# Both feed-forward products of a decoder layer by Strassen's scheme of seven block products

## What is computed

```python
hf = rmsnorm(x, norm_ffn_g[l])
gu = hf @ w_ffn_in[l]              # (1024 x 1024) @ (1024 x 5632)
gt, up = gu[..., :D_FF], gu[..., D_FF:]
x = x + (jax.nn.silu(gt) * up) @ w_ffn_out[l]   # (1024 x 2816) @ (2816 x 1024)
return rmsnorm(x, norm_final_g)
```

## Time and profile before

| | |
|---|---|
| median of 3 runs | 1623.27 us (1623.26 to 1623.52) |
| the profiled execution | 1621.26 us, of which 1619.4 us are the span from first to last instruction |
| TensorE busy | 1585.3 us, 98% of the span |
| VectorE, ScalarE, GpSimd busy | 651.1 us (40%), 450.5 us (28%), 128.9 us (8%) |
| feed-forward part | 867.0 us to the last matmul at about 1612.2 us |
| mean granted TensorE clock | 0.997 of full speed |

### The profile page before, as it was taken

The page is one execution under the profiler, slowest core; times in us unless marked ns, Lnnn a source line. Parts: engine busy times, 40 slices in busy tenths (PEclk is TensorE's granted clock), DMA queues, the critical chain, the costliest instruction groups (busy, mean ns, idle before and its releaser), DMA issues.

```text
span 1619.4 us, 18734 instructions
## 1 busy us (share of the span) xinstructions
PE 1585.3 (98%) x7640; PEld 1282.6 (79%) x7640; DVE 651.1 (40%) x916; ACT 450.5 (28%) x699; POOL 128.9 (8%) x141
## 2 busy tenths in 40 slices
PE   6999999999999999999999999999999999999998
PEld 5788888778787888887778888888888888888886
DVE  4162612666754323265636222414224142241426
ACT  5224112655643222154414211111111111111112
POOL 4000000000000002040002101010010100101002
PEclk9999999999999999999999999999999999999999
DMA  7223555323013525132011111111111111111102
GB/s 182 52 47 52 64 106 82 62 40 53 27 27 48 96 78 208 53 91 79 14 39 40 55 50 52 39 52 43 48 52 39 52 43 47 52 39 52 47 31 104
DMA packets 108538, 98.65 MB, mean 61 GB/s; under 512 B 3128, under 2 KB 90680, under 8 KB 108480
## 3 DMA queue, kind: packets, MB, share of 16 engines
q1 hardware_dynamic: 102720, 77.34, 21.2%
q0 software_dynamic: 4464, 15.77, 2.8%
q10 hardware_dynamic: 1296, 4.72, 0.7%
HBM read 89.40 MB, written 8.42 MB: 60 GB/s over the span
## 4 chain that ended last, share of the span: by engine, by line
PE 91%; DMA 2%; DVE 2%; ACT 2%; POOL 1%; issue 1%; SPq 0%; ACTq 0%; DVEq 0%; POOLq 0%
PE ps L1225 28%; PE ps L1226 28%; PE ps L1227 28%; PE ps L1475 2%; PE ps L1424 2%; PE ps L1455 1%; DMA za_dram<-za 1%; PE ps L1456 1%; DMA w_raw<-in_w_in 1%; PE ps L1232 1%; POOL w_lo L390 1%; ACT w_hi L474 0%; POOL rstd L382 0%; POOL ms L379 0%; DVE k L827 0%
## 5 line engine op out<-in xcount | busy, mean ns | idle before, releaser
L816 DVE TENSOR_TENSOR w_lo<-w_raw,w_hi 128x1024 fp32r<-128x1024 f32 (+1 forms) x124 | 151.5, 1222 | 674.2 <-ACT w_hi L474 673.0
L474 ACT ACTIVATE w_hi<-w_raw 128x1024 fp32r<-128x1024 f32 x132 | 139.4, 1056 | 882.8 <-PE ps L1227 868.8
L1225 PE MATMUL ps<-hf_lo,w_hi 128*128 128x512 f32 (+1 forms) x712 | 280.8, 394 | 0.1
L1227 PE MATMUL ps<-hf_hi,w_lo 128*128 128x512 f32 (+1 forms) x712 | 280.4, 394 | 0.0
L1226 PE MATMUL ps<-hf_hi,w_hi 128*128 128x512 f32 (+1 forms) x712 | 280.4, 394 | 0.0
L1225 PE MATMUL ps<-h_lo,w_hi 128*128 128x512 f32 (+1 forms) x456 | 183.7, 403 | 4.7 <-POOL w_lo L390 2.7
L1227 PE MATMUL ps<-h_hi,w_lo 128*128 128x512 f32 (+1 forms) x456 | 179.7, 394 | 0.0
L1226 PE MATMUL ps<-h_hi,w_hi 128*128 128x512 f32 (+1 forms) x456 | 179.4, 393 | 0.0
L1059 DVE TENSOR_TENSOR xr<-ps,xr 128x512 f32<-128x512 f32 x192 | 130.0, 689 | 88.4 <-PE ps L1227 88.4
L1225 PEld LDWEIGHTS ps<-hf_lo,w_hi 128*128 128x128 f32 x712 | 134.1, 188 | 32.1 <-issue 0.3
L1227 PEld LDWEIGHTS ps<-hf_hi,w_lo 128*128 128x128 f32 x712 | 134.1, 188 | 32.0
(11 more groups left out here) (218 smaller groups left out, 2120.7 us busy)
## 6 DMA issues: line engine op xcount, KB each, us to landing
w_raw<-in_w_ffn_in SPq DMA_DIRECT2D x44, 512.0 KB, 3.8
w_raw<-in_w_in SPq DMA_DIRECT2D x33, 512.0 KB, 7.8
w_raw<-in_w_ffn_out SPq DMA_DIRECT2D x22, 512.0 KB, 3.6
x_in<-in_x SPq DMA_DIRECT2D x8, 512.0 KB, 9.8
za_dram<-za ACTq DMA_DIRECT2D x8, 512.0 KB, 10.8
negc<-negc_dram POOLq DMA_DIRECT2D x8, 512.0 KB, 4.9
za_e<-za_dram POOLq DMA_DIRECT2D x8, 512.0 KB, 3.9
w_raw<-in_w_out SPq DMA_DIRECT2D x8, 512.0 KB, 3.6
```

Source lines behind the costliest of these rows:

```text
L474: nc.scalar.activation(w_hi[n % SLOTS][:, 0:w], w_raw[n % RAWS][:, 0:w], ACT.Copy).then_inc(hi_ready, 1)
L816: nc.vector.tensor_tensor(w_lo[n % SLOTS][:, 0:w], w_raw[n % RAWS][:, 0:w], w_hi[n % SLOTS][:, 0:w].bitcast(FP32), ALU.subtract).then_inc( ...
L1225: nc.tensor.matmul(dst, w_h, x_l, start=start, stop=False)
L1227: return nc.tensor.matmul(dst, w_l, x_h, start=False, stop=stop)
```

## The change

Both feed-forward products are cut into 2 x 2 blocks and made of seven block products for eight (Strassen's scheme, in the form with few additions). The contraction and the tokens are halved for the first product; for each of 22 column groups g of 256 (gate and up in turn) there are seven products P1, P2, P3, P7, P5, P6, P4 of 4 x 3 matmuls of 512 columns: 154 products, 1848 matmuls. For the second product there are seven sums over 11 steps, each step of 12 matmuls: 77 steps, 924 matmuls. 2772 matmuls in all.

- The token operands (B11, B21, B22 and the sums T3, T1, T2, T4) are formed once. GpSimd makes four sums for each of four pairs of token tiles, and TensorE transposes 28 units of four 128 x 128 tiles, 112 transposes, with GpSimd's `tok_t` and four PSUM banks in rotation.
- The weight operands: of seven for each g, three are quarters of the loaded pair and four are sums that GpSimd makes (`w_sums`), in one buffer `w_sum`. Each is split on ScalarE (`operand_hi`) and VectorE (`operand_lo`) seven products ahead, in a ring of ten slots.
- VectorE combines the seven results of each g (`evict`: seven operations that read PSUM), ScalarE copies P1 out. Silu and the product of gate and up work on SBUF (`silu_of`, `multiplied`). GpSimd makes four sums of the hidden quarters (`hidden_sums`), and SyncE stores seven quarters of 256 KB for each of 11 hidden blocks to DRAM (`store_hidden`, `hs_dram`). Before VectorE may overwrite `hq` for the next block, it waits for that store (`hs_stored`).
- The second product loads a hidden quarter (256 KB) for each of 77 steps (`load_hidden`, four buffers) and holds all of `w_ffn_out` in SBUF (`load_quad`); GpSimd makes 44 weight sums in place. Both operands of a step are split on ScalarE and VectorE (`split2_hi`, `split2_lo`); VectorE combines the seven sums (`evict2`, 48 operations of 128 x 512).
- The residual leaves SBUF: ScalarE issues eight stores of 512 KB while it squares (`xr_dram`) and four loads of 1 MB in the second product (`xf`).
- The hardware loops are gone; all steps are written out.

```diff
...
+OPS = ("B11", "B21", "B22", "T3", "T1", "T2", "T4")
+P1, P2, P3, P7, P5, P6, P4 = range(7)
+PAIRS_F = 2 * NJ
+ORDER = ([(0, P1), (0, P2), (1, P1), (1, P2)] + [(0, q) for q in range(2, 7)] + [(1, q) for q in range(2, 7)]
+         + [(g, q) for g in range(2, PAIRS_F) for q in range(7)])
+NTH = {gq: n for n, gq in enumerate(ORDER)}
...
+RING = 10
+LEAD = 7
...
+STEPS = PROD2 * NJ
+GROUPS = ((0, 4), (4, 8), (8, 11))
+SLOTS2 = 4
+BANKS2 = ((2, 3, 4, 6), (0, 1, 5, 7))
+T_AT = ("B11", "B22", "B12", "B12", "B11", "B12", "B21")
...
-            with sp.Fori(0, (NB - 1) // 2) as i:
-                for o in range(2):
-                    for r in range(6):
-                        n = base_of(1 + o) + r
...
+            def load_pair(g):
+                if g >= 2:
+                    sp.wait_ge(op_lo, NTH[g - 2, P4] + 1)
+                    sp.wait_ge(s_sum, 4 * (g - 2) + 4)
+                elif g == 1:
+                    sp.wait_ge(lo_ready, C_FF)
+                else:
+                    sp.wait_ge(xn_ready, N_FFN)
+                c0 = (g // 2) * 2 * P + (g % 2) * DFF
+                for half in range(2):
+                    view = w_ffn_in[half * HALF:(half + 1) * HALF, c0:c0 + 2 * P].rearrange("(k p) n -> p k n", p=P)
+                    sp.dma_start(raw_of(g, half)[:, :, :], view).then_inc(pair_in[g % 2][half], 16)
+            def store_hidden(j):
+                sp.wait_ge(hid_ready, 4 * (j + 1))
+                sp.dma_start(hs_dram[j, :, 0:3, :], hq[:, 0:3, :]).then_inc(hs_stored, 16)
+                sp.wait_ge(h_summed, 4 * (j + 1))
+                sp.dma_start(hs_dram[j, :, 3:7, :], h_sum[:]).then_inc(hs_stored, 16)
+            for g in range(PAIRS_F):
+                load_pair(g)
+                if g >= 5 and g % 2:
+                    store_hidden((g - 5) // 2)
+            store_hidden(NJ - 2)
+            def load_quad(q, i):
+                two_, col = {"B11": (0, 0), "B12": (0, 1), "B21": (1, 0), "B22": (1, 1)}[q]
+                sp.wait_ge(prod_done, N_PROD - {"B11": 5, "B22": 4, "B12": 1, "B21": 0}[q])
+                a, b = GROUPS[i]
...
+            def load_hidden(n):
+                i, k = divmod(n, NJ)
+                if n >= SLOTS2:
+                    sp.wait_ge(s_split, n - SLOTS2 + 1)
+                else:
+                    sp.wait_ge(op_lo, N_PROD)
+                    sp.wait_ge(s_sum, 4 * PAIRS_F)
+                sp.wait_ge(hs_stored, 32 * (k + 1))
+                sp.dma_start(s_raw(n % SLOTS2), hs_dram[k, :, S_AT[i], :]).then_inc(s_in[n % SLOTS2], 16)
+            ahead = {0: ("B11", 0), 2: ("B11", 1), 3: ("B11", 2), 4: ("B22", 0), 7: ("B22", 1), 9: ("B22", 2),
+                     12: ("B12", 0), 15: ("B12", 1), 18: ("B12", 2), 24: ("B21", 0), 28: ("B21", 1), 32: ("B21", 2)}
+            for n in range(STEPS):
+                if n == NJ - 1:
...
+            def w_sums(g):
+                for half in range(2):
+                    pool.wait_ge(pair_in[g % 2][half], 16 * (g // 2 + 1))
+                if g:
+                    pool.wait_ge(op_lo, NTH[g - 1, P6] + 1)
+                a11, a21 = raw_of(g, 0)[:, :, 0:P], raw_of(g, 0)[:, :, P:]
+                a12, a22 = raw_of(g, 1)[:, :, 0:P], raw_of(g, 1)[:, :, P:]
+                s3, s2, s4, s1 = (by_k(w_sum[:, i, :]) for i in range(4))
+                nc.gpsimd.tensor_tensor(s3, a11, a21, ALU.subtract).then_inc(s_sum, 1)
+                pool.wait_ge(s_sum, 4 * g + 1)
+                nc.gpsimd.tensor_tensor(s2, a22, s3, ALU.subtract).then_inc(s_sum, 1)
+                pool.wait_ge(s_sum, 4 * g + 2)
+                nc.gpsimd.tensor_tensor(s4, a12, s2, ALU.subtract).then_inc(s_sum, 1)
+                nc.gpsimd.tensor_tensor(s1, s2, a11, ALU.add).then_inc(s_sum, 1)
+            def hidden_sums(j):
+                pool.wait_ge(hid_ready, 4 * (j + 1))
+                if j:
+                    pool.wait_ge(hs_stored, 32 * j)
+                a11, a22, a12, a21 = (hq[:, i, :] for i in range(4))
+                s3, s2, s4, s1 = (h_sum[:, i, :] for i in range(4))
+                nc.gpsimd.tensor_tensor(s3, a11, a21, ALU.subtract).then_inc(h_summed, 1)
...
+                t3, t1, t2, t4 = (tok_t[:, i, :] for i in range(4))
+                nc.gpsimd.tensor_tensor(t3, x22, x12, ALU.subtract).then_inc(t_sum, 1)
+                nc.gpsimd.tensor_tensor(t1, x12, x11, ALU.subtract).then_inc(t_sum, 1)
...
+            w_sums(1)
+            w_sums(2)
+            for j in range(NJ):
+                if 2 * j + 3 < PAIRS_F:
+                    w_sums(2 * j + 3)
+                hidden_sums(j)
+                if 2 * j + 4 < PAIRS_F:
+                    w_sums(2 * j + 4)
...
+            def operand_hi(n):
+                g, q = ORDER[n]
+                if n >= RING:
+                    act.wait_ge(prod_done, n - RING + 1)
+                elif n < 6:
+                    act.wait_ge(w_used, C_XO + 2 + n // 2)
+                else:
+                    act.wait_ge(unit_done, 28)
+                if q in (P1, P2, P4):
+                    act.wait_ge(pair_in[g % 2][0 if q == P1 else 1], 16 * (g // 2 + 1))
+                else:
+                    act.wait_ge(s_sum, 4 * g + {P7: 1, P6: 2, P3: 3, P5: 4}[q])
+                nc.scalar.activation(by_k(slot_hi[n % RING]), operand(g, q), ACT.Copy).then_inc(op_hi, 1)
...
+                act.dma_start(xr_dram[t], xr[:, t, :]).then_inc(xr_stored[t // 4], 16)
...
+            def split2_hi(n):
+                i, k = divmod(n, NJ)
+                if n >= SLOTS2:
+                    act.wait_ge(step_done, n - SLOTS2 + 1)
+                else:
+                    act.wait_ge(prod_done, NTH[PAIRS_F - 1, P7] + 1)
+                    act.wait_ge(op_lo, N_PROD)
+                act.wait_ge(s_in[n % SLOTS2], 16 * (n // SLOTS2 + 1))
...
+                if n >= 2 and n + LEAD < N_PROD:
+                    operand_hi(n + LEAD)
+                if n >= N_PROD - SLOTS2:
+                    split2_hi(n - (N_PROD - SLOTS2))
...
+                    act.dma_start(xf[:, 4 * a:4 * a + 4, half_of(half)],
+                                  xr_dram[4 * a:4 * a + 4, :, half_of(half)].rearrange("t p n -> p t n")).then_inc(xf_in[i], 16)
...
+            def operand_lo(n):
+                dve.wait_ge(op_hi, n + 1)
+                minus_hi(by_k(slot_lo[n % RING]), operand(*ORDER[n]), by_k(slot_hi[n % RING]), op_lo)
...
+            def evict(g, q):
+                j, up = divmod(g, 2)
+                c11, c22, c21, c12 = ((hq if up else gbuf)[:, i, :] for i in range(4))
+                p1 = p1_sb[g % 2][:]
+                if q == P2:
+                    dve.wait_ge(prod_done, NTH[g, P2] + 1)
+                    dve.wait_ge(p1_ready, g + 1)
+                    if up and j:
+                        dve.wait_ge(hs_stored, 32 * j)
+                        dve.wait_ge(h_summed, 4 * j)
+                    nc.vector.tensor_tensor(c11, bank_of(g, P2), p1, ALU.add).then_inc(ev, 1)
+                    if up:
+                        multiplied(j, 0, EV["C11", g])
+                if q == P6:
+                    dve.wait_ge(prod_done, NTH[g, P6] + 1)
+                    nc.vector.tensor_tensor(u2_sb[:], bank_of(g, P6), p1, ALU.add).then_inc(ev, 1)
+                    dve.wait_ge(ev, EV["U2", g])
+                    nc.vector.tensor_tensor(u3_sb[:], bank_of(g, P7), u2_sb[:], ALU.add).then_inc(ev, 1)
+                    nc.vector.tensor_tensor(u2_sb[:], bank_of(g, P5), u2_sb[:], ALU.add).then_inc(ev, 1)
+                    dve.wait_ge(ev, EV["U3", g])
+                    nc.vector.tensor_tensor(c22, bank_of(g, P5), u3_sb[:], ALU.add).then_inc(ev, 1)
+                    dve.wait_ge(ev, EV["U4", g])
+                    nc.vector.tensor_tensor(c12, bank_of(g, P3), u2_sb[:], ALU.add).then_inc(ev, 1)
+                    if up:
+                        multiplied(j, 1, EV["C22", g])
+                        multiplied(j, 3, EV["C12", g])
+                if q == P4:
+                    dve.wait_ge(prod_done, NTH[g, P4] + 1)
+                    nc.vector.tensor_tensor(c21, u3_sb[:], bank_of(g, P4), ALU.subtract).then_inc(ev, 1)
+                    if up:
...
+            def split2_lo(n):
+                i, k = divmod(n, NJ)
+                dve.wait_ge(s_split_hi, n + 1)
+                minus_hi(s2_lo[n % SLOTS2][:], s_raw(n % SLOTS2), s2_hi[n % SLOTS2][:], s_split)
+                dve.wait_ge(t_split_hi, n + 1)
+                minus_hi(t2_lo[n % SLOTS2][:], wq[T_AT[i]][:, k, :], t2_hi[n % SLOTS2][:], t_split)
...
+            for n, (g, q) in enumerate(ORDER):
+                if n >= N_PROD - SLOTS2:
+                    split2_lo(n - (N_PROD - SLOTS2))
+                evict(g, q)
+                if n >= 2 and n + LEAD < N_PROD:
+                    operand_lo(n + LEAD)
...
+            def product(n):
+                g, q = ORDER[n]
+                pe.wait_ge(op_lo, n + 1)
+                if n < 4:
+                    pe.wait_ge(unit_lo, 8)
+                elif n < 8:
```

(101 more changed lines are left out.)

432 lines of the change are left out of this document (247 added, 185 removed).

## The result

| | before | after |
|---|---|---|
| median of 4 runs | 1623.39 us (1623.26 to 1623.70) | 1548.88 us (1545.92 to 1550.15) |
| ratio, 95% interval | | 0.9538 [0.9522, 0.9555] |
| profiled execution; its span | | 1550.12 us; 1548.3 us |

What follows compares the result with a forecast made beforehand. TensorE alone was taken to set the feed-forward time, other engines having room. -92.6 + 6.1 (transposes) + 18.5 + 9 + 3.9 = -55.1 on a span of 1619.4 gave 1564.3, as median 1568 us, range 1545 to 1605.

Steps and rivals of the forecast that it cites:

- 396 matmuls fewer at 0.2339 us: Feed-forward products: 3168 - 2772 matmuls removed, each priced at this trace's distance between matmuls: -92.6 us.
- Steady first product, nothing: First product once running: work of VectorE, ScalarE, GpSimd and DMA hides behind TensorE's 39.3 us per pair, costing nothing.
- Opening, +18.5: Way into the first product: squares with stores, then GpSimd's token sums delay TensorE; fifth product at 907 us, +18.5 us.
- Second product, +9: Second product: three places cost TensorE time: its start 3, transfers and load issues 4, a late combination 2 us.
- entry: Start of the second product: first weights and hidden quarters must load and be split before TensorE begins, 3 us.
- step 55: Second product: TensorE waits here for VectorE's twentieth combination, 2 us (0 to 5).
- End, +3.9: After the last matmul: four tiles complete at once, then additions, squares, scaling and store take 11.1 us for 7.2.
- The opening is cheap: Rival, chance 0.08: store issues at 0.33 us and no stall in the second product, 10 + 9 us less, 1549 us.
- Two engines exclude each other: Rival, chance 0.12: GpSimd and VectorE block each other; if for all 32 VectorE operations, 20 to 30 us more, 1595.
- The second product starves: Rival, chance 0.11: its 19.5 MB pass at 177 to 250 GB/s for 291 wanted, 11 to 43 us more, about 1595.
- The hidden store decides: Rival, chance 0.07: hidden store lands 31 us after P4, TensorE stands 10.8 us in ten pairs, +108 us, 1676 us.
- limit of 20.3 us: First product: latest landing of the hidden store after P4 that delays nobody; landing itself forecast at 9.9 us.

Runs made afterwards that it cites:

- padding runs: Unused bytes kept ahead of the placed tensors: kernel after with 32, 96, 224, 352 bytes 1541.03, 1523.33, 1539.73, 1522.80 us; kernel before with 96 bytes 1584.96 us.
- open_ab: Kernel after, with token sums of rounds 1 and 3 written over normalised values no longer read, and VectorE making four low parts earlier: 1541.23 us, 0.9501.
- two store runs: Kernel after with one more 1 MB store of hidden sums per block: beside the counted store 1558.61 us; landing before the counted store is issued 1578.02 us.
- doubled sums: Kernel after with GpSimd making each of a pair's four weight sums twice, same values written again: 1571.63 us, 0.9680.

## Why the prediction was right, and where its size was off

The spans differ by 1548.3 - 1564.3 = -16.0 us, and the profiled execution stands above the median by 1.2 us where before it stood 2.0 below. Term by term against the span:

- **396 matmuls fewer at 0.2339 us: the price was mis-sized.** It was applied to the 2772 that remain as well. From the fifth product (905.53) to the end of the first product (1322.27) 150 products take 2.778 us each, not 2.807: -4.3. The 77 steps take 212.1 us, 2.0 of them stalls: 2.728 each, -6.1. Together -10.4; the padding runs show that operand addresses do this. The Trainium skill's 215.7 ns ("TensorE: Matmul & The Clock Gate", section "Wait — 56ns, not 53.3ns?") isn't reached here: the best steady distance of any run was 226 to 227 ns.
- **Steady first product, nothing: right.** No idle time in 395 us, and taking VectorE's wait away changes nothing. But the parts were too small. An even share of the window (a pair is 14 x 2.778 = 38.9 us, so 10.16 pairs) gives VectorE 27.0 us a pair for 22.1 and GpSimd 17.8 for 15. GpSimd's sums took 1.30 to 1.75 us for 1.25, and in the chain below VectorE's subtractions take 1.7 us beside GpSimd, where 0.69 is the undisturbed time. The rule of the Trainium skill ("GPSIMD Engine Reference", Key points) that the two engines contend when VectorE has two SBUF inputs agrees with it.
- **Opening, +18.5: too dear by 4.6, which a later start hid.** The fifth product was forecast for 907 us, and came at 905.5: luck. The forecast starts at 864.8, where the projection ahead ended in the kernel before; here it ended at 867.9. The stages ahead, put at nothing, took 3.1 us more in this execution, and 0.4 us more in that of `open_ab`. From the projection's end the opening took 37.6 us for 42.2. The stores behind the squares cost 0.33 us each (issue row below), so the last square began at 868.8 and ended at 870, the lower bound, not 877. The first product started 7.6 us after the projection's end, for 15.7, at half clock as said (427 ns between matmuls), and the three rounds after the first took 7.3 us each, not 6.2. The `open_ab` run shows that the waiting of GpSimd and TensorE for each other was some 6 us of it.

```profile
L955 ACTq DMA_DIRECT2D xr_dram<-xr x8: 326/326/327, 856.4 to 868.8; - x8
```

- **Second product, +9: too dear by 6.** The entry is 0.96 us from last start to first start, 0.7 us over the usual, for 3: the loads came early although the DMA share was 0.87. The four loads of 1 MB cost no visible stall for the 4 allowed. The only stalls inside are four of some 0.5 us near 1429 to 1440 (around step 40, not at step 55), from VectorE. The chain of waits there (start, length, what):

```profile
1432.81 1.71 DVE s_lo L1053
1434.52 1.70 DVE t_lo L1053
...
1437.91 1.72 DVE t_lo L1053
1439.63 0.14 issue
```

Two subtractions at 1.7 us exceed the step of 2.73 us while GpSimd sums beside them; the prediction had priced them at 0.69. This is the place where its rival of the two engines came true, for 2 us.
- **End, +3.9: 2 us short.** 13.1 us from the end of the last matmul to the end of the span. The four squares start 1.24 us apart as forecast, but the scale of each of the last two tiles is made on GpSimd beside VectorE's scaling of a tile before, and takes 1.42 us for 0.55:

```profile
1539.73 1.06 ACT L662 ACTIVATE junk_o<-xf 128x1024 f32<-128x1024 f32 x1
...
1540.48 1.42 POOL L508 TENSOR_TENSOR rstd<-ms,minus_half 128x1 f32<-128x1 f32 x1
...
1542.26 1.42 POOL L508 TENSOR_TENSOR rstd<-ms,minus_half 128x1 f32<-128x1 f32 x1
1543.78 1.28 DVE L1049 SCALAR_TENSOR_TENSOR y_out<-xf,rstd,gain_f 128x1024 f32<-128x1024 f32 x1 [0.50 <-POOL rstd L508]
```

Sum of the errors: -10.4 (distance), +3.1 (stages ahead), -4.6 (opening), -2 (entry), -4 (inside the second product), +2 (end) = -15.9 of -16.0. Two slips in the working change nothing: 48 transposes at 0.13 us are 6.2 us, not 6.1, and the 884 us for the last square count seven stores where the formula beside it writes eight.

**The rivals.** *The opening is cheap* names nearly the measured time (1549), but not its reasons: its short issues and its unstalled second product came, its early fifth product (897) did not; the rest is the distance. *Two engines exclude each other* is real at the level of single operations and cost some 4 us (second product, end) and part of the opening's longer rounds, where GpSimd's sums took up to 2.29 us for 1.28; it did not cost the first product anything. *The second product starves* did not happen. *The hidden store decides* did not happen by 6 us: the two store runs and the doubled sums each closed that gap and paid for it.

**Left open.** Why equal addresses modulo 256 are faster; the price of the 48 more transposes alone, which no run separates from the opening; and how much of the 3.1 us ahead of the opening belongs to the change, since the profiled executions of kernels with the same stages ahead differ there by up to 2.8 us.

## What to carry to other kernels

Take the distance between matmuls for each pair of operand places, not one mean for the trace: where the moving and the stationary operand lay at the same offset modulo 256 bytes, a matmul of 512 fp32r columns took 3% less here, and one line of padding gave 26 us of 1549 (and 36 of 1621 in the kernel before). When a change also moves data, run the old kernel with the new placement before crediting the algorithm: 11 to 13 of these 74.5 us were placement. For a wait that is hidden, work out the latest harmless end as well as the cover: the limit of 20.3 us held to a fraction of a microsecond, while the guess of where the kernel stands was 4 us off, mostly because the store left its queue 3.3 us later than forecast.
